# One of three conditioning parts of the first stream multiplied and added up on VectorE instead of TensorE

## The chip, the core and the metric

One NeuronCore of a Trainium2 chip runs the whole program. The metric is the device time of one execution in microseconds, the median of several runs. Inside the core TensorE (PE), VectorE (DVE), ScalarE (ACT), GpSimd (POOL) and the queue of SyncE (SP, which issues most transfers) run side by side and meet at semaphores.

## The reference

A transformer block pair on 256 tokens of width 2048, in float32. The first block projects the normed tokens by `w_in` (the first stream), runs a sparse attention and a recurrent mixer, and a mixture of experts. The second block takes its scales and shifts from a conditioning vector:

```python
c_act = jax.nn.silu(c)                       # (1, 2048)
mod = c_act @ w_ada[l] + b_ada[l]            # w_ada: 2048 x 12288
sh1, sc1, g1, sh2, sc2, g2 = jnp.split(mod[:, None, :], 6, axis=-1)
```

`mod` has six parts of 2048 columns. Each is the product of one row of 2048 numbers with a 2048x2048 matrix of 16 MB. It depends on nothing of the first block, so the kernel computes parts 0, 1 and 2 while the first stream runs. Part 0 is the one that the change touches.

## The kernel before

**The first stream** (`first_stream`) multiplies the tokens by `w_in` in 24 column blocks of 314 columns, with 4 chunks of 512 rows in each: 96 chunks, each cut in two halves, so 192 halves. A chunk is a transfer of 628 KB into one of 4 slots of the ring, `ring.load` on SP, and the load of chunk m is held until TensorE is done with chunk m-4. ScalarE rounds each half to its high part (L276), VectorE subtracts that to get the low part (L286, called lo below), and TensorE multiplies by three passes, 12 matmuls of 314 columns a half (L302). The split tiles hold four halves: ScalarE may work on half h+4 as soon as TensorE is done with half h.

**Ticks.** Each engine's program of the stream calls `tick()` once a half (SP twice a chunk). The side work is written as generators that yield the tick at which their next piece is to stand in the engine's order. At tick h TensorE has issued half h and VectorE the lo of half h+4. All engines are strictly in order, so a piece whose input is late holds back everything behind it. SP reaches tick t when TensorE has done half t (half t-1 where t is even).

**The side work.** `SparseAttention` starts its index part at tick 42: SP waits there until 5 finished blocks of the projection are stored (`in_dram`), then loads the index queries and keys back (L2958 to L2961). From tick 46 VectorE rotates them (L3127 to L3137) one operation of 128x512 a tick, with three small ones a tick for the keys, and at tick 62 it scales the weights (L3158) and raises `ready`. TensorE waits for `ready` at tick 63 (L1960).

**The conditioning.** `Modulation.spares` hands the stream 48 loads of `w_ada` of 1 MB each, called spares below, 16 for each of parts 0, 1 and 2, through two tiles in turn (`in_spare` and the free end of the ring). At tick 9 + 15j/4 TensorE multiplies spare j, 128 rows by 2048 columns, in 4 matmuls of 512 columns (L569), each on its own 32 columns of the array, and adds over the 16 spares of a part in bank 7. SP issues the load of spare j one tick after the use of spare j-2. ScalarE copies the sum out (L618) after the last one.

Of the kernel before, what the change touches and what calls it, by code (L numbers as in the profile page):

```python
# [18 lines left out]
ALU = mybir.AluOpType  # L19
# [3 lines left out]
P = 128  # L23
D = 2048
S = 256
T = S // P
KT = D // P
RING = 8
FEW = 4
KC = 4  # L30
NB = 512
# [12 lines left out]
W1 = IN1 // 24  # L44
# [477 lines left out]
class Modulation:  # L522
# [18 lines left out]
    SPARE = 48  # L541

    def spares(self, st, tiles, conditioned):

        self.tiles, self.conditioned = tiles, conditioned
        self.filled, self.spent = [st.sem(f"filled{n}") for n in range(2)], st.sem("spent")

    def spare_tick(self, j):
        return 9 + 15 * j // 4

    def spare_sync(self, sp):
        for j in range(self.SPARE):
            yield max(0, self.spare_tick(j - 2) + 1)
            if j >= 2:
                sp.wait_ge(self.spent, j - 1)
            sp.dma_start(self.tiles[j % 2], self.source(0, j)).then_inc(self.filled[j % 2], 16)

    def spare_tensor(self, pe):
        nc = self.chip.nc
        for j in range(self.SPARE):  # L560
            part, k = divmod(j, KT)
            yield self.spare_tick(j)
            if j == 0:
                pe.wait_ge(self.conditioned, 1)
            if k == 0 and part:
                pe.wait_ge(self.copied, part)
            pe.wait_ge(self.filled[j % 2], 16 * (j // 2 + 1))
            for b in range(4):
                mm = nc.tensor.matmul(self.bank(part)[32 * b:32 * b + 32], self.c(k), self.tiles[j % 2][:, b],  # L569
                                      start=(k == 0), stop=(k == KT - 1))  # L570
            mm.then_inc(self.spent, 1)

    def spare_scalar(self, sc):
        for part in range(self.SPARE // KT):
            yield self.spare_tick(part * KT + KT - 1) + 1
            sc.wait_ge(self.spent, part * KT + KT)
            self.row_out(sc)

    def spared(self):
        self.used = self.loaded = self.SPARE  # L580

# [2668 lines left out]
def first_stream(chip, pool, sums, qkT, actT, gain, weights, dst, first_row, ada):  # L3250
# [11 lines left out]
    with Stage(chip, "in1") as st:  # L3262
# [6 lines left out]
        def in_dram(engine, n):  # L3269
            for q in range(2):  # L3270
# [4 lines left out]
                        flat[:, FEW * KC * W1:FEW * KC * W1 + 4 * NB].rearrange("p (b n) -> p b n", n=NB)), conditioned)  # L3275
        with nc.Block() as block:
            @block.sync
            def _(sp):
# [13 lines left out]
                sp.wait_ge(ada.spent, ada.SPARE)  # L3292
# [52 lines left out]
            def _(ve):  # L3345
                tick = Ticks(da.vector(ve))
# [11 lines left out]
        ada.spared()  # L3358
# [129 lines left out]
```

## Time and profile before

| | us |
|---|---|
| median of 3 runs | 3296.0 (3292.58 to 3298.17) |
| the profiled execution | 3297.05, its span 3294.8 |
| TensorE busy | 3102.6 (94%) |
| VectorE busy | 2068.0 (63%) |
| ScalarE busy | 1509.7 (46%) |
| first stream | first matmul of it at 20.70, last at about 446 |

A busy engine in the table is one with an instruction under way; idle time is put down to what released the engine. The clock is TensorE's as granted, in parts of full speed.

### The profile page before, as it was taken

The page shows a single profiled execution, that of the slowest core. Times are in us where ns is not written, and L with a number is a line of the kernel's source. Part 1 is how long each engine was busy: PE and PEld are TensorE (multiplying, and loading weights), DVE is VectorE, ACT ScalarE, POOL GpSimd, SP SyncE. Part 2 cuts the span into 40 slices and gives each one's busy share as a digit, 9 for nine tenths or more (in the row PEclk, how much of TensorE's full clock was granted, in tenths as well). Part 3 has the DMA queues.
Part 4 walks back from the last instruction along what each step waited for, and adds up shares of the span by engine and source line. Part 5 has one row for each costly group of instructions (what it writes and reads, how often), then busy time and mean ns, then how long its engine had stood idle before and what let it go on. Part 6 is the DMA issues. An engine that isn't in the chain of part 4 may idle for free. (4 is left out here: it accounts for less than half of the span.)

```text
span 3294.8 us, 43832 instructions
## 1 busy us (share of the span) xinstructions
PE 3102.6 (94%) x17864; PEld 2460.5 (75%) x17864; DVE 2068.0 (63%) x2331; ACT 1509.7 (46%) x1819; POOL 20.0 (1%) x10
## 2 busy tenths in 40 slices
PE   8999978978899999999999988999998999999997
PEld 7888846956677676667688876787776788888886
DVE  4557546354777778685548857765575655555665
ACT  4345422233556556564444465455444344444443
POOL 0000002000000000000000000000000000000000
PEclk9999978989899999999999999999999999999998
DMA  7989776086788879695376653475665655555552
GB/s 270 330 272 333 270 251 272 12 321 223 288 289 292 289 260 335 242 327 179 116 239 212 220 184 129 161 241 173 237 227 189 216 186 185 190 184 185 189 181 76
DMA packets 358321, 739.09 MB, mean 224 GB/s; under 512 B 19977, under 2 KB 118422, under 8 KB 344583
## 3 DMA queue, kind: packets, MB, share of 16 engines
q1 hardware_dynamic: 342916, 711.64, 62.9%
q10 hardware_dynamic: 15236, 25.06, 2.0%
q8 instruction: 122, 2.00, 0.3%
q14 instruction: 47, 0.39, 0.0%
HBM read 710.00 MB, written 26.65 MB: 224 GB/s over the span
## 5 line engine op out<-in xcount | busy, mean ns | idle before, releaser
L286 DVE TENSOR_TENSOR moe_w_lo<-ring,moe_w_hi 128x1024 fp32r<-128x1024 f32 x384 | 464.0, 1223 | 174.5 <-ACT moe_w_hi L276 165.5
L286 DVE TENSOR_TENSOR mx_w_lo<-ring,mx_w_hi 128x1024 fp32r<-128x1024 f32 (+1 forms) x288 | 347.5, 1210 | 308.2 <-ACT mx_w_hi L276 304.1
L276 ACT CAST moe_w_hi<-ring 128x1024 fp32r<-128x1024 f32 x384 | 402.7, 1050 | 284.6 <-PE psum L302 280.8
L276 ACT CAST mx_w_hi<-ring 128x1024 fp32r<-128x1024 f32 (+1 forms) x288 | 297.6, 1038 | 448.2 <-PE psum L302 431.9
L286 DVE TENSOR_TENSOR mlp_w_lo<-ring,mlp_w_hi 128x1024 fp32r<-128x1024 f32 x256 | 313.5, 1225 | 293.1 <-ACT mlp_w_hi L276 292.0
L276 ACT CAST mlp_w_hi<-ring 128x1024 fp32r<-128x1024 f32 x256 | 268.8, 1051 | 417.5 <-PE psum L302 417.5
L302 PE MATMUL psum<-mx_w_hi,mx_a_hi 128*128 128x496 f32 (+1 forms) x1024 | 405.4, 396 | 6.9 <-DVE mx_w_lo L286 5.2
L302 PE MATMUL psum<-mx_w_hi,mx_a_lo 128*128 128x496 f32 (+1 forms) x1024 | 397.5, 388 | 0.0
L302 PE MATMUL psum<-mx_w_lo,mx_a_hi 128*128 128x496 f32 (+1 forms) x1024 | 397.5, 388 | 0.0
L286 DVE TENSOR_TENSOR in_w_lo<-ring,in_w_hi 128x628 fp32r<-128x628 f32 x192 | 155.4, 813 | 185.7 <-ACT in_w_hi L276 184.1
L302 PE MATMUL psum<-in_w_hi,in_a_hi 128*128 128x314 f32 x768 | 244.1, 318 | 2.0 <-DVE in_w_lo L286 1.2
L276 ACT CAST in_w_hi<-ring 128x628 fp32r<-128x628 f32 x192 | 136.0, 717 | 227.1 <-PE psum L302 167.4
L302 PEld LDWEIGHTS psum<-mx_w_hi,mx_a_hi 128*128 128x128 f32 x1024 | 192.8, 188 | 59.2 <-issue 12.5
L302 PE MATMUL psum<-in_w_hi,in_a_lo 128*128 128x314 f32 x768 | 236.0, 307 | 0.0
L302 PE MATMUL psum<-in_w_lo,in_a_hi 128*128 128x314 f32 x768 | 235.4, 307 | 0.0
L302 PEld LDWEIGHTS psum<-mx_w_hi,mx_a_lo 128*128 128x128 f32 x1024 | 192.7, 188 | 38.8
L302 PEld LDWEIGHTS psum<-mx_w_lo,mx_a_hi 128*128 128x128 f32 x1024 | 192.9, 188 | 35.7
L302 PE MATMUL psum<-mlp_w_hi,mlp_heT_hi 128*128 128x512 f32 x512 | 203.1, 397 | 3.9 <-DVE mlp_heT_lo L1888 3.9
L302 PE MATMUL psum<-mlp_w_lo,mlp_heT_hi 128*128 128x512 f32 x512 | 202.9, 396 | 0.0
L302 PE MATMUL psum<-mlp_w_hi,mlp_heT_lo 128*128 128x512 f32 x512 | 202.6, 396 | 0.0
L302 PE MATMUL psum<-mlp_w_hi,mlp_a_hi 128*128 128x512 f32 x512 | 201.3, 393 | 1.4 <-DVE mlp_a_lo L249 1.4
L302 PE MATMUL psum<-mlp_w_hi,mlp_a_lo 128*128 128x512 f32 x512 | 199.7, 390 | 0.0
(596 smaller groups left out, 5605.7 us busy)
## 6 DMA issues: line engine op xcount, KB each, us to landing
ring<-in_w_ada SPq DMA_DIRECT2D x72, 1024.0 KB, 9.2
ring<-in_w_e_gate SPq DMA_DIRECT2D x64, 1024.0 KB, 5.4
ring<-in_w_e_up SPq DMA_DIRECT2D x64, 1024.0 KB, 6.4
ring<-in_w_e_down SPq DMA_DIRECT2D x64, 1024.0 KB, 5.2
ring<-in_w_up SPq DMA_DIRECT2D x64, 1024.0 KB, 5.2
ring<-in_w_down SPq DMA_DIRECT2D x64, 1024.0 KB, 5.1
ring<-in_w_in SPq DMA_DIRECT2D x64, 992.0 KB, 5.2
ring<-in_w_in SPq DMA_DIRECT2D x96, 628.0 KB, 5.5
```

The source lines that it names most:

```text
L276: self.nc.scalar.copy(self.w[0][:, self._half(j, half), :, 0:cols], self.view[:, slot, ks, 0:cols]).then_inc(self.hi_done, 1)
L286: self.nc.vector.tensor_tensor(self.w[1][:, q, :, 0:cols], self.view[:, j % self.slots, ks, 0:cols], self.w[0][:, q, :, 0:cols].bitcast(F3 ...
L302: mm = self.nc.tensor.matmul(out(t), a, w, start=(first and k == n == 0), stop=(last and k == self.HALF - 1 and n == len(passes) - 1))
```

## The change

Part 0 leaves TensorE. SP loads a spare of part 0 as 512 rows by 512 columns, in the shape 128x4x512: runs of 2 KB instead of 8 KB, still 1 MB. VectorE multiplies each of its four 128x512 pieces by the matching column of the activated vector (a number per partition) and adds it to `acc` (L599 for the first piece of each four spares, L602 for the others), two pieces at each of two neighbouring ticks: 64 operations in all. Four times, once for each 512 columns, TensorE then sums `acc` over the partitions with one matmul against 32 columns of ones, seven ticks after the tick of the last of the four spares (26, 41, 55 and 70). The spares' ticks become 9 + 29j/8, and five more from spare 16 on; the load of a spare after one of part 0 comes four ticks behind that one's tick instead of one.

```diff
     def spare_tick(self, j):
-        return 9 + 15 * j // 4
+        return 9 + 29 * j // 8 + (5 if j >= KT else 0)
...
     def spare_sync(self, sp):
...
-            yield max(0, self.spare_tick(j - 2) + 1)
+            yield max(0, self.spare_tick(j - 2) + (4 if j >= 2 and self.by_vector(j - 2) else 1))
...
+    def spare_vector(self, ve, conditioned):
...
+            b, c = divmod(j % KT, KC)
+            acc = self.acc[:, blocks % 2]
+            for half in range(2):
+                yield self.spare_tick(j) + 1 + half
...
+                for k in (2 * half, 2 * half + 1):
+                    w, m = self.tiles[j % 2][:, k], self.chip.cols[:, at + c * KC + k:at + c * KC + k + 1]
+                    if c == k == 0:
+                        ins = nc.vector.tensor_scalar(acc, w, m, None, ALU.mult)
+                    else:
+                        ve.wait_ge(self.added, n)
+                        ins = nc.vector.scalar_tensor_tensor(acc, w, m, acc, ALU.mult, ALU.add)
+                    ins.then_inc(self.added, 1)
+                    n += 1
...
+            ve.sem_inc(self.weighed, 1)
...
     def spare_tensor(self, pe):
...
+            if not self.by_vector(j):
+                yield self.spare_tick(j)
+                self.spare_use(pe, j)
+                continue
...
+            yield self.spare_tick(j) + 7
...
+            pe.wait_ge(self.weighed, n)
+            self.chip.nc.tensor.matmul(self.bank(part)[32 * b:32 * b + 32], self.chip.c("ones")[:, 0:32],
+                                       self.acc[:, blocks % 2], start=True, stop=True).then_inc(self.summed, 1)
...
-                tick = Ticks(da.vector(ve))
+                tick = Ticks(da.vector(ve), ada.spare_vector(ve, conditioned))
```

VectorE's order from tick 45 on, where the rotations begin (`pro_pool<-ring,in_csi` is one, `in_w_lo` the lo of a half). Before:

```order
L286 TENSOR_TENSOR in_w_lo<-ring,in_w_hi 128x628 x47
L3127 TENSOR_TENSOR pro_pool<-ring,in_csi 128x16x32
L286 TENSOR_TENSOR in_w_lo<-ring,in_w_hi 128x628
L3129 TENSOR_TENSOR pro_pool<-ring,in_csi 128x512
L286 TENSOR_TENSOR in_w_lo<-ring,in_w_hi 128x628
```

And in the changed kernel, the same place:

```order
L286 TENSOR_TENSOR in_w_lo<-ring,in_w_hi 128x628 x3
L3203 TENSOR_TENSOR pro_pool<-ring,in_csi 128x16x32
L602 SCALAR_TENSOR_TENSOR in_acc<-in_spare,cols,in_acc 128x512 x2
L286 TENSOR_TENSOR in_w_lo<-ring,in_w_hi 128x628
L3205 TENSOR_TENSOR pro_pool<-ring,in_csi 128x512
L602 SCALAR_TENSOR_TENSOR in_acc<-in_spare,cols,in_acc 128x512 x2
```

Between one lo and the next there now stand, on ten of the sixteen ticks of the rotations, two more operations of 128x512.

SP's order around tick 42, where it waits for the stored blocks (`ring<-in_w_in` is a chunk of the stream, `ring<-proj` the index queries). Before:

```order
L175 DMA ring<-in_w_in 128x4x314
L2958 DMA ring<-proj 128x2x1024
L2960 DMA in_ki<-proj 128x2x64 x2
L2961 DMA in_w<-proj 128x2x16
L175 DMA ring<-in_w_in 128x4x314
L556 DMA ring<-in_w_ada 128x2048
```

And in the changed kernel:

```order
L175 DMA ring<-in_w_in 128x4x314 x2
L3034 DMA ring<-proj 128x2x1024
L3036 DMA in_ki<-proj 128x2x64 x2
L3037 DMA in_w<-proj 128x2x16
L576 DMA in_spare<-in_w_ada 128x4x512
L175 DMA ring<-in_w_in 128x4x314 x2
```

A spare's load has moved ahead of the chunk that follows the wait; that chunk is number 25, whose first half is the lo of tick 46.

## Rows read from the trace of the kernel before

**Rows 1.** The page: busy us, share of the span, instructions of each engine.

```profile
PE 3102.6 (94%) x17864; PEld 2460.5 (75%) x17864; DVE 2068.0 (63%) x2331; ACT 1509.7 (46%) x1819; POOL 20.0 (1%) x10
```

**Rows 2.** Stretches: us, busy time (x instructions) of engines, clock, DMA share, GB/s.

```profile
0.00:440.00 440.00, 421.35 (x2898) 364.66 (x2899) 242.36 (x402) 200.76 (x384) 0.21 (x4) 1.00 0.84 289
...
60.00:110.00 50.00, 50.00 (x346) 42.82 (x345) 19.83 (x25) 18.68 (x27) 0.00 (x0) 1.00 0.93 320
...
119.60:152.60 33.00, 31.98 (x221) 27.63 (x220) 23.48 (x42) 13.25 (x21) 0.00 (x0) 1.00 1.00 364
```

**Rows 3.** Timeline of TensorE at four spares and after one: start, us, instruction.

```profile
54.17 1.06 PE L569 MATMUL psum<-in_spare,cols 128*32 128x512 f32 x8
55.17 0.41 PE L302 MATMUL psum<-in_w_hi,in_a_hi 128*128 128x314 f32 x1
...
62.31 1.06 PE L569 MATMUL psum<-ring,cols 128*32 128x512 f32 x8
...
70.44 1.06 PE L569 MATMUL psum<-in_spare,cols 128*32 128x512 f32 x8
...
76.83 1.06 PE L569 MATMUL psum<-ring,cols 128*32 128x512 f32 x8
```

**Rows 4.** Timeline of TensorE late in the stream, two logits matmuls of 256 columns.

```profile
396.98 1.03 PE L3021 MATMUL psum<-pro_qkT 128*128 128x256 f32 x4
397.84 0.61 PE L3034 MATMUL psum<-pro_pool 128*128 128x128 f32 x4
```

**Rows 5.** Timeline of VectorE in the rotations and the scores.

```profile
125.67 0.81 DVE L286 TENSOR_TENSOR in_w_lo<-ring,in_w_hi 128x628 fp32r<-128x628 f32 x1 [3.15 <-ACT in_w_hi L276]
126.40 0.69 DVE L3131 TENSOR_TENSOR pro_pool<-pro_pool 128x512 f32<-128x512 f32 x1
127.12 0.81 DVE L286 TENSOR_TENSOR in_w_lo<-ring,in_w_hi 128x628 fp32r<-128x628 f32 x1
...
133.11 0.22 DVE L3127 TENSOR_TENSOR pro_pool<-in_ki,in_csi 128x64 f32<-128x64 f32 x1
133.37 0.22 DVE L3129 TENSOR_TENSOR pro_pool<-in_ki,in_csi 128x64 f32<-128x64 f32 x1
...
236.14 0.48 DVE L3171 SCALAR_TENSOR_TENSOR ring<-ring,in_w 128x256 f32<-128x256 f32 x1
236.66 0.48 DVE L3173 SCALAR_TENSOR_TENSOR ring<-ring,in_w 128x256 f32<-128x256 f32 x1
```

**Rows 6.** Groups of VectorE by shape: count, busy us, mean ns, idle before.

```profile
L1665 DVE SCALAR_TENSOR_TENSOR actT<-actT,rt_share,psum 128x512 f32<-128x512 f32 x8 | 5.6, 743 | 0.0
...
L471 DVE TENSOR_SCALAR pro_pool<-pro_pool,in_n_rs 128x512 f32<-128x512 f32 x8 | 3.3, 482 | 0.0
...
L3242 DVE SCALAR_TENSOR_TENSOR ring<-psum,in_barred 128x512 f32<-128x512 f32 x4 | 2.7, 684 | 0.0
```

**Rows 7.** Timelines of ScalarE, SP and VectorE from tick 40 to tick 46.

```profile
104.41 0.72 ACT L276 CAST in_w_hi<-ring 128x628 fp32r<-128x628 f32 x1 [1.69 <-PE psum L302]
...
111.45 0.37 SPq L2958 DMA_DIRECT2D ring<-proj  x1
...
113.56 0.48 SPq L175 DMA_DIRECT2D ring<-in_w_in  x1
...
118.91 1.34 ACT L276 CAST in_w_hi<-ring 128x628 fp32r<-128x628 f32 x2 [3.93 <-DMA ring<-in_w_in]
...
119.66 0.81 DVE L286 TENSOR_TENSOR in_w_lo<-ring,in_w_hi 128x628 fp32r<-128x628 f32 x1 [3.84 <-ACT in_w_hi L276]
...
124.85 0.72 ACT L276 CAST in_w_hi<-ring 128x628 fp32r<-128x628 f32 x1 [4.02 <-DMA ring<-in_w_in]
```

**Rows 8.** Timelines of VectorE and TensorE at ticks 46, 50 and 63.

```profile
115.89 1.06 PE L569 MATMUL psum<-in_spare,cols 128*32 128x512 f32 x8
...
125.06 0.41 PE L302 MATMUL psum<-in_w_hi,in_a_hi 128*128 128x314 f32 x1
...
152.25 0.17 DVE L3158 TENSOR_SCALAR in_w<-in_w 128x32 f32<-128x32 f32 x1
...
152.54 0.66 PE L1960 MATMUL psum<-const,pro_pool 128*128 128x128 f32 x4 [1.02 <-DVEq L3159]
```

**Rows 9.** DMA issues of 60 to 150 us: KB each, median us to landing.

```profile
ring<-in_w_in SPq DMA_DIRECT2D x22, 628.0 KB, 6.7
ring<-in_w_ada SPq DMA_DIRECT2D x6, 1024.0 KB, 7.8
```

**Rows 10.** A TensorE wait later in the run, and the stretch behind it as in rows 2.

```profile
2571.33 1.93 PE L1810 MATMUL psum<-const,mlp_he 128*128 128x128 f32 x8 [4.84 <-DVE mlp_he L1882]
...
2570.00:2583.00 13.00, 11.67 (x49) 9.85 (x50) 9.46 (x7) 3.90 (x5) 0.00 (x0) 0.87 0.31 99
```

More of the change, by code:

```diff
@@ L551, in spare_sync, with by_vector, sums @@
+    def by_vector(self, j):
+        return j // KT in self.BY_VECTOR
+    def sums(self, st):
+        self.acc = st.sb("acc", [P, 2, NB])
+        self.weighed, self.summed, self.added = (st.sem(f"c_{n}") for n in ("weighed", "summed", "added"))
     def spare_sync(self, sp):
+        turns = {True: 0, False: 0}
+        of = []
         for j in range(self.SPARE):
-            yield max(0, self.spare_tick(j - 2) + 1)
+            yield max(0, self.spare_tick(j - 2) + (4 if j >= 2 and self.by_vector(j - 2) else 1))
@@ new lines, in spare_load, with spare_use @@
+    def spare_load(self, sp, j):
+        sp.dma_start(self.tiles[j % 2], self.source(0, j)).then_inc(self.filled[j % 2], 16)
+    def spare_use(self, pe, j):
+        nc, (part, k) = self.chip.nc, divmod(self.base + j, KT)
+        if k == 0 and part:
+            pe.wait_ge(self.copied, part)
+        pe.wait_ge(self.filled[j % 2], 16 * (j // 2 + 1))
+        for b in range(4):
+            mm = nc.tensor.matmul(self.bank(part)[32 * b:32 * b + 32], self.c(k), self.tiles[j % 2][:, b],
+                                  start=(k == 0), stop=(k == KT - 1))
+        mm.then_inc(self.spent, 1)
@@ L558, in spare_tensor @@
     def spare_tensor(self, pe):
-        nc = self.chip.nc
+        blocks, n = 0, 0
         for j in range(self.SPARE):
[L561 to L565, printed above, removed]
-                pe.wait_ge(self.copied, part)
[L567 to L571, printed above, removed]
+            part, q = divmod(j, KT)
+            if not self.by_vector(j):
+                yield self.spare_tick(j)
+                self.spare_use(pe, j)
+                continue
+            b, c = divmod(q, KC)
+            n += 1
+            if c < KC - 1:
+                continue
+            yield self.spare_tick(j) + 7
+            if b == 0 and part:
+                pe.wait_ge(self.copied, part)
+            pe.wait_ge(self.weighed, n)
+            self.chip.nc.tensor.matmul(self.bank(part)[32 * b:32 * b + 32], self.chip.c("ones")[:, 0:32],
+                                       self.acc[:, blocks % 2], start=True, stop=True).then_inc(self.summed, 1)
+            blocks += 1
@@ L577, in spare_scalar, with spared @@
             self.row_out(sc)
-    def spared(self):
-        self.used = self.loaded = self.SPARE
+    def spared(self, n):
+        self.used = self.loaded = self.base + n
     def begin(self):
@@ L3357, in first_stream @@
         ring.used(1, body, FEW)
-        ada.spared()
+        ada.spared(ada.SPARE)
 def load_order(d):
```

48 lines of the change are left out of this document (39 added, 9 removed).

## The prediction, made before the changed kernel ran

> **What bounds the kernel now.** I read the page's busy times first: TensorE works 94% of the span, VectorE 63% [rows 1]. That average says nothing of the place of the change, so I read the stretches of the first stream next: from 0 to 440 us TensorE is busy 421.35 us at full clock, VectorE 242.36 [rows 2]. TensorE bounds the stream, and what is taken off it there would come off the time, since the next stage begins when the stream is through. But two others stand close. The transfers are at 0.93 of their time from 60 to 110 us, moving 320 GB/s, and at 1.00 from 119.6 to 152.6, moving 364. And VectorE in that last stretch is busy 23.48 us of 33. So the question is whether ticks 9 to 65, where part 0 is done, have the room on VectorE and in the transfers, and I followed the timelines of all engines from tick 40 to tick 63.
>
> **What TensorE is spared.** Two spares with four halves between them start 8.13 us apart (62.31 to 70.44), two with three halves 6.39 (70.44 to 76.83) [rows 3]. So a half is 1.74 us, and a spare 8.13 - 4 x 1.74 = 1.17 us, of which 1.06 is matmul. Sixteen go.
>
> **What TensorE gets.** Four sums, each one matmul of 512 columns. The trace has none like it. From below it is the pair of 256 columns, 512 in all, which holds TensorE from 396.98 to 397.84, 0.86 us [rows 4]; from above a whole spare, 1.17, four times as many columns. Above, because the four matmuls of a spare take 1.06 us together and the pair of half their width 1.03 [rows 3, 4]: so the four run side by side, and one alone takes as long. I take 1.17, as the switch into 32 columns and back is in it. The Trainium skill (TensorEngine Tiling (Array Packing), Key Properties) has this as a rule: tiles of the array work independently, and a change of the tiling mode drains it. Whoever overlooks it counts a sum as a quarter of a spare, 0.3 us; the trace agrees with the page.
>
> Twelve spares net: 12 x 1.17 = **14.0 us less work on TensorE**. By tick 63 it is 15 spares less 3 sums, the same 14.0; the last spare and the last sum cancel. The 32 spares of parts 1 and 2 stay as they are, a tick or three later.
>
> **What VectorE gets.** 60 operations scalar_tensor_tensor of 128x512 and 4 tensor_scalar. The nearest row with a factor per partition takes 743 ns, one with a constant 684 [rows 6]. Each waits for the one before: at 256 columns such a pair is 0.52 us from start to start for 0.48 of duration [rows 5], so add 0.04. I take 0.78 us each and, from 482 ns for a tensor_scalar of this size [rows 6], 0.52 for those four. A spare is 3.1 us, part 0 is 49 us.
>
> **Ticks 9 to 45 have the room.** A lo takes 0.73 us from start to the next start (125.67 to 126.40) [rows 5]. In 3.625 ticks VectorE has 3.1 + 3.6 x 0.73 = 5.7 us of work, TensorE 3.6 x 1.74 = 6.3. The two heavy ticks (0.73 + 1.56 = 2.29 us against 1.74) put VectorE 1.1 us back, and the lead of three halves, 5.2 us less the cast and the lo, takes that.
>
> **Ticks 46 to 62 have not.** The rotations stand there too. From the first lo of tick 46 until `ready` VectorE must do: 17 lo at 0.73 = 12.4; 12 rotations at 0.72 (126.40 to 127.12) = 8.6; 4 ticks of three small ones at 0.26 = 3.1 [rows 5]; the scale, 0.2; and five spares, 19 x 0.78 + 0.52 = 15.3. Together **39.6 us**, without one wait. TensorE from the end of half 46 to tick 63 needs 17 x 1.74 + one sum = 30.8. And TensorE waits for `ready` at tick 63. Already before it waits there 1.02 us, `ready` coming at 152.4 [rows 8]. So the end of the stream is no longer set by TensorE's work but by when VectorE can begin tick 46, plus 39.6.
>
> **When VectorE begins tick 46.** ScalarE's cast at 104.41 marks the end of half 40. SP gets past its wait for the stored blocks at 111.45, 7.0 us later; that is the way of block 4 through cast, store and landing, and doesn't shorten. Chunk 25 is issued only then (113.56), lands at 118.9, and the lo of tick 46 starts at 119.66 [rows 7], though TensorE had done half 46 at 115.9 [rows 8]. In the changed kernel half 40 ends 9 spares less 1 sum earlier, 8 x 1.17 = 9.4: at 95.0. SP is past its wait at 102.0. Now the load of a spare goes ahead of chunk 25: 1.05 MB, at the 364 GB/s of that stretch [rows 2] 2.9 us. So chunk 25 lands at 102.0 + 7.4 + 2.9 = 112.3, the lo starts at 113.1, and `ready` comes at **152.7**. Before it was 152.4. VectorE and the late chunk eat the whole gain of 14.0 us.
>
> The bounds. If chunk 25 came in time, the lo would start 0.8 us after half 46, which ends at 95.0 + 6 x 1.74 + 1.17 = 106.6: `ready` at 147.0, 5.4 us gained. With the lower prices too (684 ns instead of 743 for 19 operations, 1.1 us, the two sums ahead of tick 46 at 0.86, 0.6 us) 7.1. If it came as late after SP's wait as chunk 26 does now behind the same spare (124.85 - 111.45 = 13.4) [rows 7], `ready` would be at 155.8, 3.4 us lost.
>
> **Behind tick 62 nothing comes back.** VectorE is three halves ahead at `ready`; spare 15 (3.1 us, ticks 64 and 65) fits into that lead, and TensorE has its three halves, 5.2 us, to do. At tick 70 ScalarE's copy waits for the last sum under 1 us, which its lead covers. SP's waits on VectorE (`weighed`) in ticks 46 to 62 come up to 6 us late and hold chunks back by some 3.5 us, but a half then takes 2.4 us, so a chunk has five of those, 12 us, for a landing of 6.7 [rows 9]. At tick 98 SP waits for stored blocks again and a spare again moves ahead of a chunk; there I take nothing, at most 2 us.
>
> **TensorE's idle time becomes one piece.** The last half that tick 63 needs is free when VectorE begins tick 59's work behind its lo; ticks 59 to 62 are about 8.5 us, less the half of 1.74 and the lo: TensorE stands some 6 us at tick 63. Later in the run a wait of 4.84 us is followed by a stretch of 13 us at 0.87 of the clock, 1.7 us lost [rows 10]. I add that 1.7.
>
> Sum: 0.3 + 1.7 = 2.0 us later, 3297.05 + 2.0 = 3299.0 for the profiled execution. That one lay 1.05 above the median of its runs, so the forecast for the median is **3298**.
>
> **Rivals.**
> *A, it is faster by the room that is left.* If chunk 25 isn't later relative to TensorE than now, the 5.4 to 7.1 us above remain: 3296 - 6 = 3290. For it speaks that SP's wait is for a store that competes with fewer bytes if TensorE is ahead; against it that a spare now stands ahead of the chunk.
> *B, VectorE never binds,* and 14.0 come off: 3282. This needs operations of under 0.35 us each, (30.8 - 24.3) / 20, and no row of two inputs with 512 columns is below 0.68.
> *C, slower: the transfers bind before VectorE does.* One tick of the new pace asks for 314 KB of chunk, 1024/3.625 = 282 of spare and 39 of store, 651 thousand bytes in 1.74 + 1.17/14.5 = 1.82 us, 358 GB/s; before it is 641 in 2.05, 313. At 320 GB/s the share is 0.93 [rows 2], so this stretch tops out at 344, 1.89 us a tick. From tick 18 to 45 that is 2 us, and the index loads of 1.1 MB are 3 more: 5 us late, where a chunk has 2 to 3 us of spare time at best, and now and then far less: the lo at 125.67 ends at 126.48 [rows 5], and TensorE, which begins half 51 at 125.06 [rows 8], wants it at 126.80. It decides once chunks land over 7 us after issue in ticks 18 to 45 (6.7 now) [rows 9]. Half 40 then ends 3 us later and so does `ready`; with the late chunk 26's 13.4 us it is 3.4 + 3 + 1.7 = 8 us: 3304.
> *D, the change does less than it says:* part 0 is computed on VectorE in the order shown, so this I exclude.
>
> A remark of the Trainium skill against the change (VectorE: DVE Perf Modes, The TRN2 errata): a float32 operation of two inputs and 512 columns takes 691 ns, with no faster mode for it. The rotations' 0.69 us agree [rows 5]. With 691 for the 19 operations `ready` comes 1.0 us earlier.
>
> **How the numbers follow.** A measurement of this kernel tells about 0.2%, 6.6 us, from no change. The forecast and what lies around it within 6.6 us: 0.64. A: 0.16, of which half beyond 6.6 us. B: 0.03. C: 0.17, nearly all beyond. That gives faster 0.11, same 0.71, slower 0.18. The range reaches from A's better bound, 3296 - 7.1 = 3288.9, to C and two more for tick 98, 3306: 3288 to 3306.
>
> **What the profile after would show.** VectorE without a gap from the lo of tick 46 to the scale, near 39.6 us, L602 near 743 ns; TensorE's wait for `ready` near 6 us instead of 1.02 and further short waits for L286 between; the lo of tick 46 held by a transfer; the four sums at 1 to 1.2 us. Wrong would be: L602 far from 0.74, or chunk 25 landing under 9 us or over 13 us after SP's wait ends, or TensorE waiting before tick 40, which is C.

## The result, and the profile after

| | before | after |
|---|---|---|
| median, measured together | 3293.45 us (7 runs) | 3305.02 us (3301.17 to 3308.38, 7 runs) |
| ratio | | 1.0031, 95% interval [1.002, 1.0043] |
| the profiled execution, its span | 3297.05, 3294.8 | 3303.38, 3301.6 |
| first load of the stage behind the stream, issued at | 449.96 | 459.08 |

The changed kernel is slower by 0.31%. That is outside the 0.2% that I had called "the same": the range of the prediction (3288 to 3306) holds the time, its forecast of 3298 does not hit it, and of the cases the nearest is C (3304). Measured against the kernel before in the same series the change costs 11.6 us, where the forecast had 2 and case C 8.

The last line of the table is the yardstick of everything below. The stage behind the stream begins when its first load is issued, so I call that moment the end of the stream. What lies behind it is the same code in every kernel here. Span less end of stream lies between 2839 and 2847 us over the 14 traces of this study, and no edit sets it: two kernels with the same late spares have 2838.9 and 2845.7. So the ledgers go by the end of the stream, and what a version is worth goes by the medians. A ledger rests on one profiled execution of each kernel, and that execution can lie up to 5 us from the median of its own kernel's runs. Here the stream ends 9.1 us later, and what lies behind it took 2.3 us less.

The busy time of the engines, from the page of the changed kernel (for [rows 1]):

```profile
PE 3093.0 (94%) x17744; PEld 2465.2 (75%) x17744; DVE 2111.1 (64%) x2395; ACT 1508.0 (46%) x1819; POOL 19.7 (1%) x10
```

TensorE is busy 9.6 us less over the run, VectorE 43 more, and the whole takes longer. The same stretches as in [rows 2]: us, busy time of each engine, clock, DMA share, GB/s:

```profile
0.00:440.00 440.00, 406.03 (x2716) 359.95 (x2716) 282.48 (x462) 196.19 (x378) 0.21 (x4) 0.98 0.83 286
60.00:110.00 50.00, 47.58 (x305) 45.05 (x304) 37.25 (x52) 19.49 (x29) 0.00 (x0) 0.97 0.94 312
...
119.60:152.60 33.00, 28.71 (x170) 25.92 (x170) 31.46 (x50) 11.27 (x17) 0.00 (x0) 0.95 0.87 289
```

Two things stand there. From 119.6 to 152.6 VectorE is busy 31.46 us of 33 (23.48 before) and TensorE 28.71 (31.98 before): VectorE has become the engine that never rests. And from 60 to 110, where VectorE has room (37.25 of 50), TensorE isn't full any more either, 47.58 in place of 50.00, with the transfers at 0.94. What TensorE waited for from 20 to 165 us, and then what SP's queue waited for (us in total, times, longest):

```profile
PE psum L302 <- DVE in_w_lo L286: 11.3, 9, 3.6
PE psum L2036 <- DVEq L3235: 5.7, 1, 5.7
```

```profile
SPq L175 <- PE psum L302: 57.5, 22, 12.2
SPq L576 <- DVEq L606: 43.8, 10, 8.2
SPq L3034 <- DMA proj<-in_out: 6.4, 1, 6.4
```

TensorE stands 17 us for VectorE where before it stood 2.2 ([rows 8] has the 1.02 of them at tick 63). SP stands 43.8 us for VectorE to give a spare's tile free (L576), which didn't exist before; whether that matters is asked below.

TensorE's three longest waits in its timeline, with the sum at tick 41 between, and last the first key product, whose short wait stands in the kernel before too (1.14 us at 165.78):

```profile
81.83 0.38 PE L302 MATMUL psum<-in_w_hi,in_a_hi 128*128 128x314 f32 x1 [2.31 <-DVE in_w_lo L286]
...
100.88 1.04 PE L639 MATMUL psum<-in_acc,const 128*32 128x512 f32 x2
...
119.64 0.41 PE L302 MATMUL psum<-in_w_hi,in_a_hi 128*128 128x314 f32 x1 [3.64 <-DVE in_w_lo L286]
...
158.61 1.11 PE L2036 MATMUL psum<-const,pro_pool 128*128 128x128 f32 x4 [5.72 <-DVEq L3235]
...
173.36 0.49 PE L3075 MATMUL psum<-in_kiT,pro_pool 64*128 64x128 f32 x4 [1.13 <-ACT in_kiT L3139]
```

and what ScalarE, SP and VectorE did there (for [rows 7] and [rows 8]):

```profile
80.13 1.33 ACT L276 CAST in_w_hi<-ring 128x628 fp32r<-128x628 f32 x2 [6.79 <-DMA ring<-in_w_in]
...
101.29 0.37 ACTq L3397 DMA_DIRECT2D proj<-in_out  x1
...
107.87 0.37 SPq L3034 DMA_DIRECT2D ring<-proj  x1
...
110.14 0.47 SPq L576 DMA_DIRECT2D in_spare<-in_w_ada  x1
...
118.02 1.33 ACT L276 CAST in_w_hi<-ring 128x628 fp32r<-128x628 f32 x2 [8.21 <-DMA ring<-in_w_in]
...
118.77 0.81 DVE L286 TENSOR_TENSOR in_w_lo<-ring,in_w_hi 128x628 fp32r<-128x628 f32 x1 [6.26 <-ACT in_w_hi L276]
...
158.33 0.17 DVE L3234 TENSOR_SCALAR in_w<-in_w 128x32 f32<-128x32 f32 x1
```

From the lo of tick 46 at 118.77 to the scale at 158.33 are 39.6 us, and VectorE has no gap in them: this is the piece that the prediction had worked out as 39.6. But it begins 5.7 us later than foretold (113.1).

Around these three waits the granted clock falls from full to half, the lower of its two levels, 1.2 GHz of 2.4. It is 0.50 in each of three stretches behind them:

```profile
83.00:84.50 1.50, 1.50 (x8) 1.50 (x7) 1.50 (x3) 0.77 (x2) 0.00 (x0) 0.50 1.06 360
120.50:123.00 2.50, 2.50 (x11) 2.27 (x10) 2.46 (x4) 0.67 (x2) 0.00 (x0) 0.50 1.05 370
160.00:164.00 4.00, 4.00 (x17) 3.96 (x17) 0.41 (x2) 1.04 (x2) 0.00 (x0) 0.50 0.40 167
```

### The profile page after: what moved, and what is told of

It reads as the page before. It is cut to its first block and busy times, and to the rows that moved or that the text cites. A ratio compares the mean times of both kernels' runs of the same rounds, so it can differ in the third digit from the quotient of the medians.

```text
span 3301.6 us, 43684 instructions
## 1 busy us (share of the span) xinstructions
PE 3093.0 (94%) x17744; PEld 2465.2 (75%) x17744; DVE 2111.1 (64%) x2395; ACT 1508.0 (46%) x1819; POOL 19.7 (1%) x10
## 5 line engine op out<-in xcount | busy, mean ns | idle before, releaser
L302 PE MATMUL psum<-in_w_hi,in_a_hi 128*128 128x314 f32 x768 | 246.9, 321 | 12.6 <-DVE in_w_lo L286 11.3
L302 PEld LDWEIGHTS psum<-mx_w_hi,mx_a_hi 128*128 128x128 f32 x1024 | 193.4, 189 | 58.7 <-issue 12.5
```

The costliest lines, as they stand in the source:

```text
L302: mm = self.nc.tensor.matmul(out(t), a, w, start=(first and k == n == 0), stop=(last and k == self.HALF - 1 and n == len(passes) - 1))
```

## The experiments

Two theories had to be told apart, and a third that would have made both needless.

- **V**, the prediction's own: VectorE can't do the rotations and the weighted sums of ticks 46 to 62 in the time, and gives the gain back there.
- **C**, its rival: TensorE's new pace asks for more than the transfers bring; chunks come late from tick 18 on, before VectorE binds anywhere.
- **H**: chunks are late because SP, in order, is held by its waits for VectorE to free a tile (the 43.8 us above), or because it issues them in a worse order.

C's own sign is in the traces. Of the chunks issued from 50 to 107 us the median lands 6.6 us after its issue in the kernel before and 7.5 us in the changed one.

Every experiment kernel is told by its difference from the changed kernel, save where the kernel before is named.

### VectorE does a quarter of its sums

```diff
-                for k in (2 * half, 2 * half + 1):
+                for k in ((0,) if half == 0 else ()):
```

> The changed kernel, but VectorE does only the first of the four operations of each spare of part 0 (48 of 64 are left out, so part 0 of mod is not what it should be); loads, waits and sums stay. Theory V (VectorE binds in ticks 46 to 62): the work from the lo of tick 46 to ready falls from 39.7 us to about 28, so tick 63 on TensorE comes some 12 us earlier than in the changed kernel (158.6) and the wait of 5.7 us there falls under 1.5; the stream ends near 443 us instead of 455, the median near 3293. Rival C (the transfers alone are short of bandwidth): the wait of 2.3 us near 82 us and the late chunk 25 stay, and the stream ends at 452 or later. Rival H (SP, held by its waits on VectorE, issues chunks late): the wait near 82 us goes too, as VectorE is done with each spare 2 us sooner, and the stream ends at 441 or before.

Measured: 3289.62 us, ratio to the kernel before 0.9983 [0.9974, 0.9993]; end of the stream 447.81, 11.3 us before the changed kernel's. The two places in TensorE's timeline:

```profile
82.32 0.38 PE L302 MATMUL psum<-in_w_hi,in_a_hi 128*128 128x314 f32 x1 [2.62 <-DVE in_w_lo L286]
...
148.53 0.85 PE L2036 MATMUL psum<-const,pro_pool 128*128 128x128 f32 x4 [2.90 <-DVEq L3235]
```

Tick 63 comes 10 us earlier, so V is real. Its wait fell to 2.90 us, not under 1.5 as theory V had it, and the stream ends between what V (443) and C (452 or later) had foretold. The wait at 82 doesn't move, with three quarters of VectorE's new work gone and SP's waits on VectorE down from 43.8 to 20.7 us. It is ended by VectorE's lo in the profile's words, but VectorE is only the last in a row: ScalarE's cast in front of it had stood 7.11 us for the chunk. That speaks for C and against H.

The clock did not follow this wait. It is longer than the changed kernel's (2.62 against 2.31 us), and the granted clock stays full behind it:

```profile
83.00:84.50 1.50, 1.50 (x12) 1.50 (x12) 1.50 (x3) 1.24 (x3) 0.00 (x0) 1.00 1.06 362
```

### The loads are left out

```diff
+            if v and j >= 2:
+                sp.sem_inc(self.filled[j % 2], 16)
-            if v:
+            elif v:
```

> The changed kernel without 14 of the 16 loads of part 0 (the tiles keep spares 0 and 1, so part 0 of mod is not what it should be); VectorE's work, SP's waits on it and the sums stay. Theory V alone: ready still comes late, at 150 or so, since 39.7 us from the lo of tick 46 stay and that lo still waits for chunk 25 behind the stored blocks; tick 63's wait on TensorE stays at 5 to 6 us. Rival C: TensorE has no wait before tick 46, half 40 ends at 95.0 as forecast instead of 99.1. Rival H: SP's waits on VectorE stay, and with them at least 1 us of TensorE's wait near 82 us. The stream ends near 447; if it ends under 443, VectorE did not bind.

Measured: 3295.01 us, ratio 0.9999 [0.9989, 1.0008]; end of the stream 447.21. The stretch 60 to 100 us, and the sum at tick 41 and tick 63 in TensorE's timeline:

```profile
60.00:100.00 40.00, 40.00 (x266) 37.95 (x265) 33.17 (x46) 17.17 (x25) 0.00 (x0) 1.00 0.73 212
```

```profile
96.50 1.04 PE L641 MATMUL psum<-in_acc,const 128*32 128x512 f32 x2
...
148.18 1.11 PE L2038 MATMUL psum<-const,pro_pool 128*128 128x128 f32 x4 [5.72 <-DVEq L3237]
```

With the transfers at 212 GB/s TensorE is full again from 60 to 100, at full clock, and the sum at tick 41 comes at 96.50 where the changed kernel has it at 100.88. So half 40 ends 4.4 us earlier, near the 95.0 that the prediction had taken. SP still waits 30.0 us for VectorE in this run, and TensorE has no wait near 82 all the same, which speaks against H. The chunks issued from 50 to 107 us land 4.3 us after their issue (median). And the wait at tick 63 is the same 5.72 us: that one needs no load to be late. All of this, and the end of the stream near 447, is as V and C together had foretold it.

### Both at once

The two edits above together.

> The changed kernel with both of the suspected costs taken away at once: 14 of the 16 loads of the first part are left out (as in the run without them), and VectorE does only the first of the four operations of each of its spares. So the weighted sums are not computed; TensorE's work is the changed kernel's. With the loads alone left out the end of the stream stood at 447.2, with the operations alone thinned at 447.8, in the changed kernel at 459.1. If either cost alone is enough to eat the gain of 14.0 us and there is no third, both gone leaves 449.96 - 14.0 + 1 (the waits at ends of rows that stay), rwkv's first load at 436 to 438, the time 3281 to 3284, and the kernel before's wait at tick 63 back to 1 to 2 us. If a third cost is in the design (the place of the sums' matmuls, the new ticks), the load comes at 440 or later.

Measured: 3282.55 us, ratio 0.9967 [0.9955, 0.998]; end of the stream 435.22. The wait at tick 63:

```profile
137.53 0.66 PE L2038 MATMUL psum<-const,pro_pool 128*128 128x128 f32 x4 [0.53 <-DVEq L3237]
```

The stream ends 14.7 us before the kernel before's, just ahead of the 436 to 438 expected: TensorE's bill of 14.0 was right by the traces, and they show no third cost. With this run the four make a square. ScalarE issues the store of a finished block once in eight halves; the table has the moment of that issue at some of them, the kernel before's in us, the others as the difference to it.

| store issued at half | before | changed (V and C) | sums thinned (C alone) | loads out (V alone) | neither | cost of V | cost of C |
|---|---|---|---|---|---|---|---|
| 24 | 70.63 | -3.0 | -1.7 | -4.6 | -4.7 | 0.1 | 3.0 |
| 40 | 104.43 | -3.1 | -3.8 | -9.5 | -9.6 | 0.1 | 5.8 |
| 48 | 124.86 | -4.9 | -6.0 | -14.9 | -14.9 | 0.1 | 8.9 |
| 56 | 137.49 | +2.9 | -1.6 | -9.7 | -12.5 | 2.8 | 10.9 |
| 64 | 155.05 | +7.9 | -2.5 | -3.1 | -15.0 | 11.9 | 12.5 |
| 128 | 300.24 | +9.2 | -2.1 | -2.7 | -14.6 | 11.9 | 12.5 |
| 192 | 446.90 | +9.1 | -2.2 | -2.8 | -14.8 | 12.0 | 12.6 |

(The cost of V is loads out less neither, that of C thinned less neither. C here is all that the loads of part 0 cost, their place in SP's order included.) V is nothing until half 48 and comes whole between 48 and 64, where the prediction had put it. C grows from half 24 to 64, 12.6 us in the end. Behind half 64 neither adds anything. The two together are 24.6, the changed kernel lost 23.9: in these traces they add up.

The medians, each against the kernel before in its own series, give smaller and less even numbers: changed +11.6 us, sums thinned -4.9, loads out +0.5, neither -11.0. By them V costs 11.5 us with the loads out and 16.5 with them in, and C costs 6.1 us with the sums thinned and 11.1 with them in full. The profiled execution of the thinned run lay 4.8 us above that run's median, more than any other here, so the C column may be several us too high. Both ways of counting agree on this much: V alone takes the gain or nearly all of it, C alone takes about half of it or more, and together they turn a gain of 11 to 15 us into a loss of 9 to 12. That is the answer to where the gain went: it was spent twice, or nearly so. Whether the two add exactly is not shown.

### A third tile

```diff
+    def tile(self, j):
+        return j % 3 if j < 15 else (j - 15) % 2
```

and a third tile of 1 MB in a free part of the stage's memory. SP then asks for a spare of part 0 only when VectorE is done with the one three before it, not two before it. At tick 42 the spare's load also comes to stand behind chunk 25.

> The changed kernel with a third tile for the spares of part 0 (in memory that is free until tick 114), so SP asks for a spare only when VectorE is done with the one three before, five ticks after its tick; at tick 42 the load of the spare then stands behind chunk 25. The bytes and VectorE's work are the same. Rival H: SP's waits on VectorE, 43.8 us in ten in the changed kernel, fall under 10 in ticks 9 to 45, TensorE's wait near 82 us goes (2.3 us and the slow clock after it, 4 us), chunk 25 lands 2.9 us earlier after SP's wait for the stored blocks; ready near 151 instead of 158.5, the stream ends near 447, median 3297. Rival C: the bytes are the same, so the wait near 82 us stays; ready near 155.5 by the order at tick 42 alone. Theory V alone: 39.7 us from the lo of tick 46 to ready stay in each case.

Measured: 3300.6 us, ratio 1.0017 [1.0007, 1.0027]; end of the stream 455.81. SP's waits on VectorE fell from 43.8 us in 10 to 14.2 in 5:

```profile
SPq L588 <- DVEq L618: 14.2, 5, 5.6
```

yet the wait near 82 is there (2.43 us at 81.67) and so is that at tick 63 (5.72). The first half of H, that SP is held by its waits on VectorE, is refuted. The stream ends 3.3 us earlier, and this comes at chunk 25: its cast starts at 114.84 in place of 118.02. The next run takes that order alone.

### One load in another order

```diff
-            yield max(0, self.spare_tick(j - 2) + (4 if j >= 2 and self.by_vector(j - 2) else 1))
+            yield max(0, self.spare_tick(j - 2) + (4 if j >= 2 and self.by_vector(j - 2) else 1) + (j == 10))
```

so that chunk 25, not spare 10, is the first load behind SP's wait for the stored blocks.

> The changed kernel with one load moved: spare 10's comes at tick 43 instead of 42, behind chunk 25 and not ahead of it. If the order was worth the 2.9 us that the prediction put on it, chunk 25 lands 7.4 us after SP's wait for the stored blocks ends instead of 10.2, ready is at 155.6 instead of 158.5 and the stream ends near 452; median some 3 us under the changed kernel's. If the transfers under way set the landing and not the order, nothing moves by over 1 us. If spare 10 then comes too late for VectorE, the gain of the lo is given back in a wait of the first L602 of tick 46.

Measured: 3302.37 us, ratio 1.0025 [1.0015, 1.0034]; end of the stream 456.30. ScalarE's cast of chunk 25:

```profile
115.15 1.34 ACT L276 CAST in_w_hi<-ring 128x628 fp32r<-128x628 f32 x2 [4.75 <-DMA ring<-in_w_in]
```

8.2 us behind SP's release (106.95) in place of 10.15 (118.02 - 107.87), so the order is worth 2.0 us there. The prediction had priced a spare in front of a chunk at 2.9 us. The stream ends 2.8 us earlier, of which 0.9 is SP's release, which the edit doesn't touch. H's second half is true, but small; by the medians the gain is about 3 us, and the interval of its ratio overlaps the changed kernel's.

### The small loads elsewhere

```diff
+        yield 30
         for j in range(2):
             sp.dma_start(self.cs[:, j], d["rope_head"]...
```

> The changed kernel with one move: the four small loads of SP's queue that it issues at tick 24 (the head tables and gains) are issued at tick 30. In the changed kernel chunk 16 is late by 6.8 us of ACT's waiting at 80 and TensorE waits 2.3 us at 81.8. If the small pieces ahead of the chunks in the ring cause it, the wait at 81.8 falls under 1 us and rwkv's first load comes 3 to 4 us before 459.08, at 455 to 456, the time 3300 to 3302. If the total demand of the stretch (theory C, 358 GB/s wanted and 322 moved) does, the wait stays at 2 us or more, there or a few ticks on, and the load at 458 to 460, the time 3304 to 3306.

Measured: 3300.95 us, ratio 1.0019 [1.001, 1.0029]; end of the stream 457.66. The wait near 82 is gone, one of 1.25 us stands at 95.6, and the clock is 1.00 from 60 to 100 (0.96 in the changed kernel). But tick 63 came at 157.65, only 1.0 us earlier than in the changed kernel, and the end of the stream moved by 1.4 us, not by 3 or 4. The time of 3300.95 is the one expected if the small loads were the cause, so the two readings disagree. TensorE's busy time from 60 to 100 hardly moved (37.87 us against 37.58). In this trace the small loads decide at which chunk the shortage shows, not whether there is one; how much they cost over many runs is open.

### Only the first ten spares on VectorE, none of it in ticks 46 to 62

From the kernel before: its ticks, its loads in rows of 8 KB, spares 0 to 9 on VectorE in two operations of 128x1024 each, one set of four sums at tick 49.

```diff
-    SPARE = 48
+    SPARE, VECTOR = 48, set(range(10))
```

> The kernel before with its 48 spare products at their old ticks (every 3.75th), the loads in rows as before, and only the first ten of them (rows 0 to 9 of the first part) on VectorE: two operations of 128x1024 for each, their running sum in pool memory, and four matmuls at tick 49 for all ten. So 10 x 1.17 - 1.17 = 10.5 us of TensorE go, and none of VectorE's new work lies in ticks 46 to 62. Theory V (after's gain was given back at tick 63 because VectorE, late by chunk 25, has 17 gapless ticks with weighted sums in them): the wait of L1960/L2036's matmul of tick 63 is again about 1 to 3 us, and the product of tick 63 comes 6 to 9 us earlier than before's 152.5. If half 40 and the waits for late chunks cost as much as in the changed kernel (some 4 us, theory C), rwkv's first load comes at 443 to 446 (before 449.96), the time is 3287 to 3291, ratio 0.998. Theory H (VectorE's work of any kind in this stretch costs TensorE as much as it takes off): rwkv's first load at 449 to 452 and no gain.

Measured: 3298.89 us, ratio 1.0008 [0.9998, 1.0018]; end of the stream 450.61. The gain of 10.5 us is gone although V can't act: tick 63 waits 0.20 us. TensorE lost it before:

```profile
80.35 0.38 PE L302 MATMUL psum<-in_w_hi,in_a_hi 128*128 128x314 f32 x1 [2.30 <-DVE in_w_lo L286]
...
114.53 1.93 PE L615 MATMUL psum<-in_spare,cols 128*32 128x512 f32 x8 [6.37 <-DMA in_spare<-in_w_ada]
```

The first of these is the changed kernel's wait near 82, in a design with other loads and other operations. That is C again, and it shows that the change's runs of 2 KB aren't needed for it: here they are 8 KB. The second I had not foreseen, and took for C too. The expected end of 443 to 446 was missed; 449 to 452 is what the expectation's theory H had, by which any VectorE work in the stream costs as much as it saves. The late spares below speak against that.

### The same with its loads left out

```diff
+            if j in self.VECTOR and j >= 2:
+                sp.sem_inc(self.filled[j % 2], 16)
```

> The version with rows 0 to 9 of the first part on VectorE, with the loads of rows 2 to 9 left out, so the sums are taken over stale tiles; everything else, VectorE's operations too, is as there. That version's load of rwkv came at 450.6, with TensorE waiting 2.3 us at 80.3 and 6.4 us at 108 to 114 for a spare's transfer, each followed by a stretch at the half clock. If transfers alone took its 10.5 us, both waits are gone (under 1 us each), the clock is 1.00 from 60 to 130, and rwkv's first load comes at 439 to 441, the time 3284 to 3287. If it stays at 445 or later, the cost was not the transfers.

Measured: 3291.24 us, ratio 0.9991 [0.9981, 1.0]; end of the stream 446.49. The wait at 80 is gone, and the store of half 40 is issued at 94.70, 9.7 us before the kernel before's. But here is SP behind its wait for the stored blocks, and TensorE at tick 46:

```profile
98.52 0.37 SPq L3014 DMA_DIRECT2D ring<-proj  x1
...
102.08 0.75 SPq L571 DMA_DIRECT2D in_spare<-in_w_ada  x1
```

```profile
110.64 1.94 PE L618 MATMUL psum<-in_spare,cols 128*32 128x512 f32 x8 [5.64 <-DMA in_spare<-in_w_ada]
```

I expected no wait over 1 us here and an end at 439 to 441; both missed. Spare 10 is TensorE's own. A tile that VectorE uses is given free four ticks after its spare, not one, so the load of spare 10 moved from tick 40 to tick 43, behind SP's wait at tick 42. The wait is short here, 1.7 us; the three ticks are 5.2. The load is issued at 102.08 and lands 8.5 us later, while TensorE wants it at 105.0. In the kernel before that load (102.44) stands ahead of the wait (111.45). So the 10.5 us of the version above went two ways: about 3.3 us to C by half 40 (98.03 against 94.70), and most of the rest to a late load that my own edit made. The second I read from the trace; no run moves that load back. By the measure set before this run (an end at 445 or later) the transfers alone did not take that version's gain.

### The late spares on VectorE

From the kernel before: spares 37 to 47 on VectorE, and from spare 38 on one each 3.5 ticks instead of 3.75. Spare 38 has tick 151 in both kernels, and spare 47 has 182 in place of 185. The expectation says that this moves them behind the scores; in fact they stood there already.

```diff
-    SPARE = 48
+    SPARE, VECTOR = 48, set(range(37, 48))
...
-        return 9 + 15 * j // 4
+        return 9 + 15 * j // 4 if j < 38 else 151 + 7 * (j - 38) // 2
```

> The kernel before with spares 37 to 47 on VectorE (two operations of 128x1024 each) and moved behind the scores' stage, where the bands are made: ten at a tick of 3.5 from tick 151 on, and spare 37 where it stood. Eleven spares of 1.17 us go from TensorE and one set of four matmuls comes: 10 x 1.17 = 11.7 us less. The rotations of the first 63 ticks have no VectorE work added before tick 147, so chunk 25, the end of tick 62 and the product of tick 63 stand where before's do (kiT 165.8, within 1.5). Theory V: VectorE has room there, rwkv's first load comes 9 to 12 us before 449.96, at 438 to 441, and the time is 3282 to 3286, ratio 0.997. If this stretch is bound by VectorE or by the transfers as the earlier one is, the stage gives back half or more: 444 or later, 3289 or more.

Measured: 3282.62 us (3281.07 to 3283.49), ratio 0.9958 [0.9942, 0.9975]; end of the stream 440.30. Up to half 144 every store is issued within 0.8 us of the kernel before's; from there the gain grows to 9.7 us. VectorE's new operation, and the stretch 300.4 to 367.8:

```profile
L588 DVE SCALAR_TENSOR_TENSOR pro_pool<-in_spare,cols,pro_pool x10: 1275/1278/1280, 351.3 to 418.2; 128x1024 f32<-128x1024 f32 x10
```

```profile
300.40:367.80 67.40, 66.26 (x467) 60.84 (x466) 50.50 (x67) 31.50 (x50) 0.00 (x0) 1.00 0.87 299
```

VectorE is busy 0.75 of this stretch and TensorE 0.98. The same idea, put where VectorE has room and in longer operations, keeps 9.7 of 11.7 us, as theory V had foretold. This is the fastest complete kernel of the study.

### Both places

Spares 0 to 9 and 37 to 47 on VectorE.

> Both of the two edits beside it: rows 0 to 9 of the first part on VectorE at their old ticks, and spares 37 to 47 on VectorE behind the scores. If the two are independent the gains add: rwkv's first load at 449.96 - 5 - 10.5, about 434 (430 to 437), time 3277 to 3282, ratio 0.996. If a later stage of the stream is bound by its transfers alone, the second adds nothing to the first and the load comes at the earlier of the two single ones, near 440.

Measured: 3288.68 us, ratio 0.9975 [0.9965, 0.9984]; end of the stream 444.08, outside the 430 to 437 expected, as the early part brought no gain to add to. The late part adds its gain here too (the difference to the kernel before goes from +4.1 at tick 64 to -5.6 at the end, 9.7 again), the early part costs more than in the run with it alone: TensorE's two waits are 3.47 and 8.49 us in place of 2.30 and 6.37, with code that is the same up to there. So at tick 64 two executions of the same code stood 3 us apart, and a difference of that size between two traces shows nothing by itself.

### All sixteen of the third part

```diff
-    SPARE, VECTOR = 48, set(range(37, 48))
+    SPARE, VECTOR = 48, set(range(32, 48))
```

(against the version with eleven).

> The version with eleven late spares on VectorE, with all sixteen of the third part there: spares 32 to 36 too, at their old ticks 129 to 144, two operations of 128x1024 each (2.56 us, measured 1.28 each). TensorE is rid of 16 x 1.17 - 1.17 = 17.5 us in place of 11.7. In 294 to 340 VectorE is busy 11.1 of 15 us, that is 6.0 per 3.75 ticks of 8.1 us, and with 2.56 on top 8.6: 0.5 us too much for each of five spares, 2 to 3 us behind at tick 148. So of the further 5.8 us some 3 stay: rwkv's first load at 436 to 438 (440.30 with eleven), time 3278 to 3281. If VectorE's delay hits TensorE in full in each spare (no slack of two ticks), it gives all 5.8 back: 440 to 442.

Measured: 3286.13 us, ratio 0.9976 [0.9967, 0.9986]; end of the stream 441.49. Five more spares off TensorE and no gain from them, the worse of the two expectations: TensorE waited 2.14 us at 337.0 and 1.54 at 346.1, and the first key product (kiT) stood 1.0 us later than before. VectorE is busy 0.92 of the stretch that it filled to 0.75 with eleven spares, and TensorE 0.91:

```profile
300.40:367.80 67.40, 61.63 (x426) 59.84 (x425) 62.05 (x77) 31.73 (x51) 0.00 (x0) 1.00 0.88 297
```

### The change itself, on the third part

The changed kernel with its operations and loads applied to part 2 instead of part 0, from tick 129 on.

```diff
-    SPARE, BY_VECTOR = 48, (0,)
+    SPARE, BY_VECTOR = 48, (2,)
...
-        return 9 + 29 * j // 8 + (5 if j >= KT else 0)
+        return 9 + 15 * j // 4 if j < 2 * KT else 129 + 29 * (j - 2 * KT) // 8
```

> The change itself, its own operations and column-block loads, applied to the third part in place of the first: parts one and two on TensorE at the ticks of the kernel before, part three on VectorE from tick 129 on at 3.625 ticks, sums seven ticks behind. TensorE's work falls by the same 16 x 1.17 - 4 x 1.17 = 14.0 us. Up to tick 129 all stands as before (kiT at 165.8). From 294 to 340 VectorE is busy 11.1 of 15 us in the kernel before, and 3.1 us per 7.8 come on top: 8.9 of 7.8, so it falls behind by about 1.1 x 6 = 6 us by tick 151, and catches up behind it (7.0 of 15 there). Theory V (what matters is VectorE's sum of busy time against the ticks' length, stretch by stretch): TensorE waits for the lo parts by 3 to 6 us there and the rest of the gain stays; rwkv's first load at 439 to 443, time 3283 to 3288. If the edit costs anywhere what it saves: 448 or later, 3293 or more.

Measured: 3291.65 us, ratio 0.9998 [0.9988, 1.0008]; end of the stream 449.21, 0.75 us before the kernel before's in place of the 7 to 11 expected. The stretch 300.4 to 367.8 in this kernel, and in the kernel before:

```profile
300.40:367.80 67.40, 61.32 (x406) 58.44 (x405) 64.72 (x89) 28.20 (x44) 0.00 (x0) 0.97 0.88 284
```

```profile
300.40:367.80 67.40, 67.40 (x478) 58.62 (x476) 41.94 (x56) 29.46 (x46) 0.00 (x0) 1.00 0.86 293
```

VectorE runs from 300.40 on without a gap over 0.15 us, 64.72 us of 67.4 in execution (the rest is between operations that wait for each other), and TensorE loses 6.1 us of work there. I read this as V without C, since VectorE never stands for a chunk there (the transfers do 284 GB/s). No run leaves the loads of this version out, so it is argued and not shown. I had let the arrears grow by 1.1 us for each of six spares and then fall; they were still growing behind tick 151, since the late products of the scores' softmax (L3123 waits for VectorE's L3311, up to 2.1 us) come on top.

## Why the prediction missed the forecast and held the range

By its own steps, in their order:

**TensorE's bill: right.** A sum by one matmul of 512 columns holds TensorE 0.97 us (69.62 to 70.59), a spare 1.00 (54.17 to 55.17 in [rows 3]). With both costs taken away 14.7 us were gained of 14.0 in the trace, 11.0 by the medians. The Trainium skill (TensorEngine Tiling (Array Packing), Key Properties) says that the tiles of the array work independently of each other. The trace agrees: one tile alone takes as long as four, and whoever prices it at a quarter is wrong by 3 us over the four sums.

**VectorE's prices: right.** 60 operations at 752 ns, 4 at 482. From start to start those of ticks 46 to 62 take 0.786 us, foretold 0.78:

```profile
L602 DVE SCALAR_TENSOR_TENSOR in_acc<-in_spare,cols,in_acc x28: 744/752/753, 44.0 to 156.7; 128x512 f32<-128x512 f32 x28
```

The 691 ns that I had weighed against my 743 (the Trainium skill, VectorE: DVE Perf Modes, The TRN2 errata) are the page's figure for tensor_tensor, not for this operation. They would have been too low: here the measurement decides.

**Ticks 46 to 62: right to the tenth.** 39.6 us foretold, 39.6 measured, without a gap, and TensorE's wait at tick 63 "some 6 us": 5.72. The terms are right one by one too, none off by more than 0.2 us.

**When VectorE begins tick 46: wrong, 113.1 foretold, 118.77 measured.** This is the step that failed, in its first term; TensorE waiting before tick 40, which the prediction had named as the mark of C, is in the trace at 81.83. "Half 40 ends at 95.0": by the sum at tick 41 (100.88 less a half of 1.74) it ended at 99.1, 4.1 us later. TensorE's time up to there was taken as its work alone, though the working of C showed 358 GB/s asked of 344: 2.31 us are the wait at 81.83, and the half clock from 82.7 to 86.1, with a matmul each 0.26 us in place of 0.145, is 1.5 more. The 344 was no steady ceiling: from 60 to 100 us the changed kernel moved 322 GB/s, less than the kernel before's 334. What the traces show is that chunks landed later, not that a fixed rate was reached. The loads-out run has half 40 at 94.8. The second term, "7.0 us from half 40 to SP, and doesn't shorten", didn't shorten, but grew to 8.8: ScalarE issued the store at 101.29, 2.2 us behind half 40, as late chunks stood before it in ScalarE's order. The third, chunk 25 behind a spare, was right: 10.3 foretold, 10.15 measured, and 2.0 of it the order.

**The clock: too small.** 1.7 us foretold for the stretch behind tick 63. From tick 63 to the first key product the changed kernel takes 14.75 us (158.61 to 173.36) and the kernel before 12.07 (152.54 to 165.78, less the spare of 1.17 that it does there): 2.7. With the loads out the same wait of 5.72 us was followed by only 2.8 us at the half clock instead of 6.0, and the same piece took 13.3 us: 1.3. So the foretold 1.7 lies between two measured costs of the same wait, and no run shows what decides.

The ledger of the stream: foretold 0.3 + 1.7 = 2.0. Measured 4.1 + 1.8 - 0.1 = 5.8 on top of the 0.3, and 1.0 more of clock: 8.8 to 9.1, and 9.1 is what the trace has.

**Rival C was true, beside the forecast and not in place of it.** I gave it 0.17 as "the transfers bind before VectorE does" and priced it 3 us at half 40; it was 4.1. I had written "and so does ready", which is how the two add: V sets tick 63 as so many us from the lo of tick 46, and C sets that lo. So the fault is one of form too. I treated C as an alternative, with its own chance, where my own numbers (a demand above what the same row allows) made it a term of the sum. With its 3 us as a term the sum gives 5.0 us and a median of 3301, which is 4 us short.

**That C's 3304 and the range's end at 3306 come so near is luck in part.** C's 8 us were 3 at half 40, 3.4 for a chunk 25 as late as chunk 26, and 1.7 of clock. The 3.4 did not happen: chunk 25 came 10.15 us behind SP's release, not 13.4. In their place stand 1.1 more at half 40, 1.8 of a later store and 1.0 of clock, none of which I had. The 2 us that the range had for tick 98 were not spent either. And the kernel before measured 3293.45 in the series with the changed kernel, 2.6 less than the 3296.0 that I had added to: the change of 11.6 us is more than any case foretold, and only the lower base keeps the time inside the range.

**Left open.** Why C costs 12.6 us by half 64 when by half 40 it costs 5.8: the spare loads of ticks 46 to 62 meet the stored blocks' loads behind SP's wait there, but no run took those alone away. How much of the 12.6 stays over many runs, where the medians give 6 to 11. And what separates two executions of the same code by 3 us in that stretch.

## What to carry to other kernels

Before work is taken off the bounding engine, work out what its new pace asks of each other engine and of the transfers, stretch by stretch; where that is above what the same rows show them to give, it belongs in the sum and not among the rivals. The ceilings act one behind the other, and one doesn't hide the other: here 12.0 and 12.6 us in the traces against a gain of 14.7, and no less than 11.5 and 6.1 against 11.0 by the medians. And the same idea was worth 0.4% in one version and nothing in others. In the stretch of 300.4 to 367.8 it paid where the helping engine was busy 0.75 of the time, new work included (9.7 of 11.7 us kept), and no longer at 0.92 or 0.96. These versions differ in the size of the operations and the number of spares as well as in place, so no run shows what place alone is worth. Room on the helping engine is not enough either: from 60 to 110 us it was busy 0.75 in the changed kernel too, and TensorE lost work to a late chunk there. And look at which tick each load is issued and when its user wants it: a load moved by three ticks cost a wait of 5.64 us.

## What the runs showed of the hardware

- The granted clock stood at 0.50 for 3.4 us (82.7 to 86.1) behind a TensorE wait of 2.31 us in the middle of full work, which cost 1.5 us more than the wait's own length. Behind a wait of 2.62 us at the same place, in the run with the sums thinned, and behind one of 2.14 us with sixteen late spares, it stayed at 1.00. Around one and the same wait of 5.72 us it stood at 0.50 for 6.8 us in the changed kernel and for 3.4 with the loads out. So a wait's length alone doesn't tell what it costs. I had counted such a loss only behind the 4.84 us of [rows 10].
- scalar_tensor_tensor with a factor per partition, float32, all operands in the same on-chip memory: 752 ns for 128x512, 1278 ns for 128x1024. The longer operation does a spare in 2.6 us in place of 3.1.
- From 60 to 100 us the transfers moved 322 to 346 GB/s in the kernels with all their loads, TensorE full or not (334 with TensorE full in the kernel before), and 212 to 215 where the spares' loads were left out. With the 212 TensorE was full and at full clock.
